# The scores multiply of an attention stage: from fp32 to two stacked fp32r halves

## The reference

```python
proj = rmsnorm(x, norm_g) @ w_in            # 1024 query columns, 48 gate columns
...
s = einsum('bghqd,bgnd->bghqn', q_c, k_cmp) * scale      # compressed
s = where(valid, s - slopes * dist, NEG)
p_cmp = softmax(s) * valid.any(-1)
...
s = einsum('bghqd,bgqkld->bghqkl', q_c, ks) * scale      # blocks
s = where(dist >= 0, s - slopes * dist, NEG)
...
s = einsum('bghqd,bgmd->bghqm', q_c, kw) * scale         # window
...
o = g_c[0] * o_cmp + g_c[1] * o_slc + g_c[2] * o_win
return out @ w_out
```

## Time and profile before

| what | value |
|---|---|
| median of 3 runs | 2514.72 us (2511.58 to 2517.59) |
| the profiled execution, its own time | 2515.49 us |
| its span | 2513.6 us, 31422 instructions |
| mean granted TensorE clock | 0.954 of full |
| busy of the span | PE 92%, PEld 70%, DVE 49%, ACT 37%, POOL 33% |
| key/value stage and attention | from about 1707 to about 2090 us of the span |

### The profile page before, as it was taken

How to read it: one execution, slowest core, us unless ns; L and a number is a source line. 1 busy time by engine, 2 the same in 40 slices (tenths; PEclk the granted TensorE clock), 3 DMA queues, 4 the chain that set the end, 5 groups by cost and what they waited for, 6 DMA issues and landing times.

```text
span 2513.6 us, 31422 instructions
## 1 busy us (share of the span) xinstructions
PE 2301.6 (92%) x10462; PEld 1770.5 (70%) x10462; DVE 1234.5 (49%) x1886; ACT 937.9 (37%) x1466; POOL 825.4 (33%) x366
## 2 busy tenths in 40 slices
PE   3899999998699999788869999999999999999997
PEld 2677777776578888655437888887655557788886
DVE  5466666643433332289964333234265565333322
ACT  4433433433444432342144443221254444444322
POOL 2522222222434444431204444445101103444442
PEclk8999999999799999989989999999699999999998
DMA  3211111112222232211102222422000001222322
GB/s 121 92 34 42 33 42 33 42 34 71 71 78 98 97 108 92 79 43 42 50 17 92 92 100 92 147 89 84 9 17 17 17 9 59 92 92 100 104 94 77
DMA packets 43689, 169.94 MB, mean 68 GB/s; under 512 B 4849, under 2 KB 4977, under 8 KB 43121
## 3 DMA queue, kind: packets, MB, share of 16 engines
q1 hardware_dynamic: 43056, 163.82, 19.5%
q10 hardware_dynamic: 576, 5.37, 0.5%
HBM read 167.08 MB, written 2.10 MB: 67 GB/s over the span
## 4 chain that ended last, share of the span: by engine, by line
PE 74%; DVE 10%; issue 9%; ACT 5%; POOL 1%; DVEq 1%; DMA 1%; ACTq 0%; POOLq 0%; SPq 0%
PE bank L282 19%; PE bank L284 19%; PE bank L283 19%; PE bank L1631 2%; PE bank L707 2%; ACT Pr L1677 2%; PE bank L699 1%; PE bank L712 1%; PE bank L1595 1%; DVE ACC L382 1%; DVE act L778 1%; PE bank L1462 1%; POOL WL L247 1%; PE bank L1613 1%; DVE Y L1365 1%
## 5 line engine op out<-in xcount | busy, mean ns | idle before, releaser
L247 POOL TENSOR_TENSOR WL<-raw,WR 128x1024 fp32r<-128x1024 f32 (+2 forms) x288 | 738.0, 2563 | 973.9 <-ACT WR L243 969.3
L282 PE MATMUL bank<-XR,WR 128*128 128x512 f32 x1528 | 631.9, 414 | 45.9 <-DVE XL L403 31.7
L284 PE MATMUL bank<-XR,WL 128*128 128x512 f32 x1528 | 603.0, 395 | 0.0
L283 PE MATMUL bank<-XL,WR 128*128 128x512 f32 x1528 | 602.0, 394 | 0.0
L243 ACT ACTIVATE WR<-raw 128x1024 fp32r<-128x1024 f32 (+2 forms) x230 | 255.7, 1114 | 739.3 <-PE bank L284 731.7
L282 PEld LDWEIGHTS bank<-XR,WR 128*128 128x128 f32 x1528 | 290.7, 190 | 123.7 <-issue 37.0
L282 PE MATMUL bank<-MR,WR 128*128 128x512 f32 (+1 forms) x856 | 336.5, 393 | 17.3 <-DVE ML L1391 8.0
L283 PEld LDWEIGHTS bank<-XL,WR 128*128 128x128 f32 x1528 | 291.9, 191 | 60.2 <-issue 7.9
L284 PEld LDWEIGHTS bank<-XR,WL 128*128 128x128 f32 x1528 | 290.6, 190 | 61.8
L283 PE MATMUL bank<-ML,WR 128*128 128x512 f32 (+1 forms) x856 | 332.9, 389 | 0.0
L284 PE MATMUL bank<-MR,WL 128*128 128x512 f32 (+1 forms) x856 | 332.8, 389 | 0.0
(11 more groups left out here) (268 smaller groups left out, 2676.6 us busy)
## 6 DMA issues: line engine op xcount, KB each, us to landing
raw<-w SPq DMA_DIRECT2D x224, 512.0 KB, 3.3
raw<-w SPq DMA_DIRECT2D x48, 704.0 KB, 4.0
raw<-w SPq DMA_DIRECT2D x16, 384.0 KB, 3.0
hT<-xT SPq DMA_DIRECT2D x1, 2048.0 KB, 8.1
hT<-xT ACTq DMA_DIRECT2D x1, 2048.0 KB, 7.8
phi<-phi ACTq DMA_DIRECT2D x1, 2048.0 KB, 8.5
out<-Y SPq DMA_DIRECT2D x8, 256.0 KB, 2.0
memT<-memT ACTq DMA_DIRECT2D x1, 1024.0 KB, 8.0
```

The source lines that it names most:

```text
L247: nc.gpsimd.tensor_tensor(WL[:, here], raw[:, here], WR[:, here].bitcast(F32), ALU.subtract).then_inc(weight_split, 1)
L282: nc.tensor.matmul(into, wr, xr(k0 + k), start=start, stop=False)
L283: nc.tensor.matmul(into, wr, xl(k0 + k), start=False, stop=False)
L284: mm = nc.tensor.matmul(into, wl, xr(k0 + k), start=False, stop=stop)
```

## The change

Lines L1407 to L1810 of the kernel. The scores multiply takes fp32r operands. A query tile is made for each pair and group, Q_S[j][g], 128 rows deep: 64 rows hold the high halves of the 64 query features, the other 64 the low halves. The keys stand doubled, once in each half of the rows, as a high tile and a low tile (KS for the full branches, KC for the compressed one). Scores are then two matmuls of 128 rows (with the high, and with the low keys) in place of one fp32 matmul of 64 rows. Q_S is made by ScalarE (two high halves, `q_scalar`) and VectorE (two low halves, `q_vector`), both behind the eviction of item 2 or 8. The key tiles are made once in the key/value stage.

The inputs to the gate and query units are multiplied by R before they are split (`q_scale` on VectorE, a high half on ScalarE, `q_low` on VectorE), so that neither the query tiles nor the gate rows need R afterwards. VectorE builds the windows before it takes the gate rows, and TensorE waits for the gate rows (tile_taken, seg_a.tile0 + 7) before the window matmuls. The gates' sigmoid and transposes move ahead of the second small layer. Buffers move to other places in SBUF.

```diff
+        KS = [[[at(f"KS{i}{g}{part}", (16 + 8 * i + 4 * g + 2 * part) * KB, SEQ, F32R) for part in range(2)]
+               for g in range(2)] for i in range(2)]
...
+            pe.wait_ge(tile_taken, seg_a.tile0 + 7)
...
-            pe.wait_ge(hid_ready, 2)
-            nc.tensor.matmul(bank[7][:, 0:32], phi2[:, 0:P], hidden[:, 0:32], start=True, stop=True)
-            nc.tensor.matmul(bank[7][0:32, 128:256], hidden[:, 32:64], phi2[:, P:2 * P], start=True, stop=True).then_inc(cmp_done, 1)
...
             pe.wait_ge(gate_sig, 1)
             for b in range(NB):
                 mm = nc.tensor.transpose(bank[2][:, b * 48:(b + 1) * 48], g_rows[0:48, b * P:(b + 1) * P], ident[0:48, 0:48])
             mm.then_inc(gate_turned, 1)
+            pe.wait_ge(hid_ready, 2)
...
-                high_part(act, "q", n, q_in_R[n], cols(hT, n), param("b_norm", n))
+                act.wait_ge(q_scaled, n + 1)
+                nc.scalar.activation(q_in_R[n], cols(SQ, n % 2), ACT.Identity).then_inc(input_high, 1)
+            act.wait_ge(unit_done, seg_a.unit0 + 6)
+            for i in range(2):
+                act.wait_ge(tile_taken, seg_a.tile0 + 3 + i)
+                for g in range(2):
+                    for rows in (HALF[g], HALF[1 - g]):
+                        nc.scalar.activation(KS[i][g][0][rows, :], k_rows[i][HALF[g], :], ACT.Identity).then_inc(keys_high, 1)
...
-            low_parts = iter(range(DT))
+
+            def q_scale(n):
+                if n >= 2:
+                    dve.wait_ge(input_ready, INPUT["q"] + n - 1)
+                V.scalar_tensor_tensor(cols(SQ, n % 2), cols(hT, n), param("b_norm", n), R[:, :], ALU.mult, ALU.mult).then_inc(q_scaled, 1)
+
+            def q_low(n):
+                dve.wait_ge(input_high, INPUT["q"] + n + 1)
+                V.tensor_tensor(q_in_L[n], cols(SQ, n % 2), q_in_R[n].bitcast(F32), ALU.subtract).then_inc(input_ready, 1)
+
+            q_scale(0)
+            q_scale(1)
...
-                for n in (next(low_parts, None), next(low_parts, None)):
-                    if n is not None:
-                        low_part(dve, "q", n, q_in_L[n], cols(hT, n), q_in_R[n], param("b_norm", n))
-            dve.wait_ge(tile_taken, seg_a.tile0 + 6)
-            dve.wait_ge(unit_done, seg_a.unit0 + 7)
-            V.tensor_tensor(g_rows[0:48, :], kv_bank(6)[0:48, :], R[0:48, :], ALU.mult).then_inc(tile_taken, 1)
+                for n in range(2 * j, 2 * j + 2):
+                    if n < DT:
+                        q_low(n)
+                        if n + 2 < DT:
+                            q_scale(n + 2)
             for i in range(2):
+                dve.wait_ge(tile_taken, seg_a.tile0 + i + 1)
                 order.link(V.memset(windows[i][:, :], 0.0))
                 out_w = windows[i][:, :].rearrange("p (l n) -> p l n", l=L_CMP)
...
+            dve.wait_ge(unit_done, seg_a.unit0 + 7)
+            V.tensor_copy(g_rows[0:48, :], kv_bank(6)[0:48, :]).then_inc(tile_taken, 1)
+            for i in range(2):
+                for g in range(2):
+                    dve.wait_ge(keys_high, 4 * i + 2 * g + 1)
+                    for rows in (HALF[g], HALF[1 - g]):
+                        V.tensor_tensor(KS[i][g][1][rows, :], k_rows[i][HALF[g], :], KS[i][g][0][HALF[g], :].bitcast(F32),
+                                        ALU.subtract).then_inc(keys_low, 1)
...
-            dve.wait_ge(cmp_done, 1)
-            V.tensor_copy(k_cmp[:, :], bank[7][:, 0:32]).then_inc(cmp_ready, 1)
-            V.tensor_copy(v_cmp[:, :], bank[7][0:32, 128:256]).then_inc(cmp_ready, 1)
...
-            pe.wait_ge(tile_taken, i * 2 + (q_tiles + j))
+            if isinstance(i, int) and i == 0 and j == 0:
+                pe.wait_ge(tile_taken, q_tiles)
+            else:
+                pe.wait_ge(q_ready, i * 4 + 2 * j)
...
-            rows = slice(64 * g, 64 * g + 64)
-            pe.wait_ge(tile_taken, i * 2 + (q_tiles + idx // N_ITEMS * 2 + j + 1))
+            pe.wait_ge(q_ready, i * 4 + (idx // N_ITEMS * 4 + 2 * j + g + 1))
             pe.wait_ge(scores_read, nth(i, idx) + 1)
...
-                    mm = nc.tensor.matmul(bank[2][:, b * 32:(b + 1) * 32], qT[j][rows, b * P:(b + 1) * P], k_cmp[rows, :],
-                                          start=True, stop=True)
+                    for part in range(2):
+                        mm = nc.tensor.matmul(bank[2][:, b * 32:(b + 1) * 32], Q_S[j][g][:, b * P:(b + 1) * P], KC[g][part][:, :],
+                                              start=part == 0, stop=part == 1)
...
-                    mm = nc.tensor.matmul(bank[2 + n][:, at0:at0 + (b + 1) * P], qT[j][rows, b * P:(b + 1) * P],
-                                          k_rows[r - 1][rows, 0:(b + 1) * P], start=True, stop=True)
+                    for part in range(2):
+                        mm = nc.tensor.matmul(bank[2 + n][:, at0:at0 + (b + 1) * P], Q_S[j][g][:, b * P:(b + 1) * P],
+                                              KS[r - 1][g][part][:, 0:(b + 1) * P], start=part == 0, stop=part == 1)
...
+            pe.wait_ge(cmp_low, 4)
             scores_tensor(pe, 0, 0)
+            pe.wait_ge(keys_low, 8)
+            pe.wait_ge(vt_ready, 2)
+            pe.wait_ge(v_cmp_ready, 1)
             scores_tensor(pe, 0, 1)
...
+        def q_scalar(act, i, j):
+            act.wait_ge(unit_done, i * 2 + (q_units + j + 1))
+            for g in range(2):
+                nc.scalar.activation(Q_S[j][g][HALF[g], :], bank[0][HALF[g], :], ACT.Identity).then_inc(q_high, 1)
...
         def q_vector(dve, i, j):
-            dve.wait_ge(unit_done, i * 2 + (q_units + j + 1))
-            nc.vector.tensor_tensor(qT[j][:, :], bank[0][:, :], R[:, :], ALU.mult).then_inc(tile_taken, 1)
+            for g in range(2):
+                dve.wait_ge(q_high, i * 4 + (2 * j + g + 1))
+                nc.vector.tensor_tensor(Q_S[j][g][HALF[1 - g], :], bank[0][HALF[g], :], Q_S[j][g][HALF[g], :].bitcast(F32),
+                                        ALU.subtract).then_inc(q_ready, 1)
...
                     evict_vector(dve, i, n)
+                    if n % 6 == 2 and exists(i, n + 6):
+                        q_vector(dve, *((i, 1) if n < 6 else (i + 1, 0)))
                     if exists(i, n + 1):
                         scale_vector(dve, i, n + 1)
                     if exists(i, n + 2):
                         read_vector(dve, i, n + 2)
-                    if n == 1:
-                        q_vector(dve, i, 1)
-                    if n == 7 and exists(i, N_ITEMS):
-                        q_vector(dve, i + 1, 0)
```

More of the change, by code:

```diff
@@ L1415, in program @@
         v_rows = [at(f"v_rows{i}", behind_r + (4 + 2 * i) * KB, SEQ) for i in range(2)]
+        KC = [[at(f"KC{g}{part}", behind_l + 128 * (2 * g + part), 32, F32R) for part in range(2)] for g in range(2)]
+        v_cmp = at("v_cmp", behind_l + 512, P, parts=32)
         v_tok = [at(f"v_tok{i}", behind_r + (8 + 2 * i) * KB, SEQ) for i in range(2)]
-        k_cmp = at("k_cmp", behind_l, 32)
-        v_cmp = at("v_cmp", behind_l + 128, P, parts=32)
-        gates = at("gates", behind_l + 640, NB * 48)
         g_rows = at("g_rows", behind_l + 2 * KB, SEQ)
         c_rows = [at(f"c_rows{i}", behind_l + (4 + 2 * i) * KB, SEQ) for i in range(2)]
+        gates = at("gates", low + 6 * KB + 32, NB * 48)
+        KS = [[[at(f"KS{i}{g}{part}", (16 + 8 * i + 4 * g + 2 * part) * KB, SEQ, F32R) for part in range(2)]
+               for g in range(2)] for i in range(2)]
         windows = [at(f"windows{i}", (32 + 4 * i) * KB, L_CMP * 32) for i in range(2)]
@@ L1471, in kv_tensor @@
             mm.then_inc(gate_turned, 1)
+            pe.wait_ge(hid_ready, 2)
+            nc.tensor.matmul(bank[7][:, 0:32], phi2[:, 0:P], hidden[:, 0:32], start=True, stop=True)
+            nc.tensor.matmul(bank[6][0:32, 128:256], hidden[:, 32:64], phi2[:, P:2 * P], start=True, stop=True).then_inc(cmp_done, 1)
         def kv_scalar(act):
@@ L1479, in kv_scalar @@
                 nc.scalar.activation(hidden[:, i * 32:(i + 1) * 32], bank[5 + i][:, 0:32], ACT.Silu).then_inc(hid_ready, 1)
-            act.wait_ge(tile_taken, seg_a.tile0 + 7)
-            nc.scalar.activation(g_rows[0:48, :], g_rows[0:48, :], ACT.Sigmoid).then_inc(gate_sig, 1)
+            act.wait_ge(cmp_done, 1)
+            for g in range(2):
+                for rows in (HALF[g], HALF[1 - g]):
+                    nc.scalar.activation(KC[g][0][rows, :], bank[7][HALF[g], 0:32], ACT.Identity).then_inc(cmp_high, 1)
         def kv_vector(dve, order):
@@ L1694, in y_scalar @@
             nc.scalar.activation(cols(MR, i * 2 + (8 + j)), bank[7][:, :], ACT.Identity).then_inc(y_high, 1)
+        def q_scalar(act, i, j):
+            act.wait_ge(unit_done, i * 2 + (q_units + j + 1))
+            for g in range(2):
+                nc.scalar.activation(Q_S[j][g][HALF[g], :], bank[0][HALF[g], :], ACT.Identity).then_inc(q_high, 1)
         def attend_scalar(act):
             alibi_scalar(act, 0, 0)
+            q_scalar(act, 0, 0)
```

(3 more changed lines are left out.)

42 lines of the change are left out of this document (26 added, 16 removed).

## The result

| | before | changed |
|---|---|---|
| median of the runs compared | 2517.74 us | 2524.11 us (2521.69 to 2536.44, 12 runs) |
| ratio, 95% interval | | 1.0036 [1.0022, 1.0049] |
| span of the profiled execution, granted clock | 2513.6 us, 0.954 | 2523.2 us, 0.947 |

The account below looks back on a forecast made before the run. VectorE's list was taken to bind the 15.36 us group, not TensorE. The span was 2513.6 - 0.1 - 4.3 + 3.5 + 6.7 = 2519.4 us, giving a forecast median of 2520.5 us, range 2507 to 2534.

Parts of the forecast that it names:

- key/value stage, to the pair unit: Making keys, windows and gates: windows +0.9, from their end to the pair unit -1.6, first pair +0.6; together -0.1 us.
- start of the attention: First work of the attention, at half clock, where TensorE binds: shorter scores give -4.3 us (ends 0 and -6).
- query halves, 7 turns: Behind each of seven pair units, making the query halves puts read(a) 0.5 us later: +3.5 us.
- clock: Weighing(a): longer TensorE waits drop the clock in six of 15 groups, four more than now, 1.68 us each: +6.7 us.
- What binds: Steady attention group of 15.36 us: VectorE's list binds; TensorE is on the path for only 3.43 us.
- TensorE bound after all: Rival, steady attention: the scores' half comes back in full, 2468 us, or half of it, about 2490; chance 0.10.
- Scores: Steady attention: scores take 1.13 to at most 1.3 us against 2.35, with 0 gained on the path.
- Compressed scores: Steady attention, ahead of weighing(a): they go from about 1.0 us to between 0.2 and 1.0, taken as 0.5.
- that sign of being right: In a steady group TensorE is idle 1.4 us or more ahead of weighing(a), ended by ACT PT.
- about 60: Sign of being right: TensorE's busy time in a steady 74 us falls to about 60 us.
- after 1755: Sign of being wrong, key/value stage: the window matmuls start before 1750 or after 1755 us.
- Nearer to the low end since each row of today shows the edge: Reason for taking six clock falls, +6.7 us, between ends of 0 of 15 (-3.4) and all (+21.8).

Follow-up runs that it names:

- c3_fill_behind: The changed kernel with four extra useless TensorE multiplies behind each weighing(c) alone; ratio to the kernel before 1.0010.
- b4_before_fill: The kernel before with three extra useless TensorE multiplies ahead of each weighing(a); ratio to the kernel before 0.9987.
- a2_before_short: The kernel before with only the scores shortened: two fp32r matmuls of 64 rows, the second overwriting the first, low halves left out; ratio 1.0014.
- a1_fill: The changed kernel with six extra useless TensorE multiplies ahead of each weighing(a) and four behind each weighing(c); ratio to the kernel before 1.0003.
- b1_qlate: The changed kernel with VectorE's low query halves moved behind the read of the same step; ratio to the kernel before 1.0040.
- b3_fill4: The changed kernel with four extra useless TensorE multiplies ahead of each weighing(a) alone; ratio to the kernel before 1.0036.
- c1_fill44: The changed kernel with four extra useless TensorE multiplies ahead of each weighing(a) and four behind each weighing(c); ratio to the kernel before 1.0012.
- c4_short_fill44: The kernel before with only the scores shortened (low halves left out), plus four extra multiplies ahead of weighing(a) and four behind weighing(c); ratio 1.0005.
- c2_qlate_fill44: The changed kernel with low query halves behind the read, plus four extra multiplies ahead of weighing(a) and four behind weighing(c); 2507.96 us, ratio 0.9973.

## Why the prediction was right, step by step

Clean group periods come from c3_fill_behind, which has no fill ahead of weighing(a) and keeps its clock in most groups: 21.45 with a pair, 15.15 without. Before: 20.79 and 15.36. The kernel before without its falls is b4_before_fill's 274.5 less 0.9 for its one slow weighing, 273.6; the changed one would be 273.6 + 7 x (0.66 - 0.21) = 276.8.

| term | forecast | measured |
|---|---|---|
| key/value stage, to the pair unit | -0.1 | -1.3 (windows +0.45, from there -1.7) |
| start of the attention | -4.3 | -5.6 |
| query halves, 7 turns | +3.5 | +3.2 |
| clock | +6.7 | (295.7 - 276.8) - (280.3 - 273.6) = +12.2 |
| sum | +5.8 | +8.5, and +1.0 of drift outside |

- *What binds*: right. VectorE's list and ScalarE's eviction set the group; less TensorE work alone gave nothing (a2_before_short), and more of it cost nothing as long as it fitted the wait: with three more multiplies b4_before_fill keeps its groups at 20.79 and 15.37. Six, in a1_fill, overshoot it and cost 0.6 and 0.44 a group (22.06 and 15.59). "TensorE bound after all" is refuted, though the page said 91% and b4_before_fill 99%.
- *Scores*: turning(b) and scores together take 1934.20 - 1931.74 = 2.46 and turning alone 1.24 (1981.62 to 1982.86), so 1.22 for the scores, as forecast (1.13 to 1.3). *Compressed scores* did not shrink: 1.06 against 1.07, where I took 0.5. Eight products of 32 columns with 128-column weights cost 0.13 each before and after, so it wasn't the passes over the columns that set it. So the idle time ahead of weighing(a) did not grow to 1.5; it is 0.97, and that sign of being right is missing. So is "about 60" for TensorE's busy time in a steady 74 us: it is 65.26 (1923.86 to 1997.86, clock 0.91), with the slow weighings in it.
- *Query halves*: +0.67 per pair group against 0.5, but 0.21 less in each other group, through the pair's split standing earlier (the last leg, 5.99 against 6.21), where I had said 0.1 at most. Most of that comes from the shorter scores, which I had put at 0: a2_before_short has 15.22 where it keeps its clock, 0.14 less than before. GpSimd did not hold them, as the row of a PSUM input had said. The Trainium skill (SBUF — State Buffer, section "SBUF: two separate sides") has the rule that a VectorE operation with both inputs in SBUF and a GpSimd operation that reads SBUF shut each other out; b1_qlate agrees, to 0.02 us.
- *Key/value stage*: the window matmuls start at 1755.78, and "after 1755" was a sign of being wrong. 3.55 of it were there before the stage began; without them it is 1752.2, as forecast (1752.7).
- *Start*: right in sign, 1.3 short. The clock is back to 1.00 at the first weighing(a) (2.37 us), which took 4.35 before; these 2.0 us stand in the clock's term.
- *Clock*: the mechanism was right, the size half of what it is. A fall costs what I took, 1.7 each (18.9 / 11, 6.7 / 4). The number failed: I counted two falls today and there were three behind the first (the third, 4.03 us, in the last turn), and took four more. Behind the first there were eight more, 11 in place of 3; the first one no longer falls, so the net is seven. "Nearer to the low end since each row of today shows the edge" was the wrong reading: standing on the edge, the place falls with the next bit of work taken away. I had named a second wait ahead of turning(a), of about 1 (it is 0.65), but counted on the one ahead of weighing(a); c3_fill_behind and b3_fill4 show that the place of the second counts more. The waits ahead of scores(b) and weighing(c) I had not seen at all. The rule of the Trainium skill (TensorE: Matmul & The Clock Gate, section "HAM oscillation — how this bites in real kernels"), by which a wait in each turn costs the clock in each turn, would have had all 15 fall: 11 did, between its 15 and my six, and the clock's 12.2 us is nearer to my 6.7 than to its 21.8. Its example waits for transfers, far longer than the 0.2 to 1.15 us of a turn here.

That the total came near is in part luck. The clock's price was half of what it is, and two things beside the right mechanism hid that: start and key/value stage gave 2.5 more than forecast against the 5.5 that the clock took more, and the medians lie 6.4 apart where the two profiled executions, from which the table is made, lie 9.5 apart.

Open: why c1_fill44 and c4_short_fill44 still fell at other places in some turns, and c2_qlate_fill44 hardly; and whether useful work can take the place of the fill. It was not tried.

## What to carry to other kernels

Walk one steady turn from mark to mark before believing that the busiest engine binds: here TensorE, 95% busy, was in 3.4 of 15.4 us of it. If it does not bind, taking work from it opens waits, and the price of those is the clock: count the slow turns of today; here four became eleven. A few useless multiplies in the waits are a one-line trial that tells what the clock costs, and may be worth keeping; count how many fit the wait, since here six cost time that four did not. And before an operation is moved out of the way, see what stall it stood in (the 1.41 us of query halves hid 1.34) and who needs its result next (moved two items on, they kept TensorE waiting 1.2 to 1.7 us).

## What the runs showed of the hardware that I had not expected

- The same line of eight multiplies takes 2.37 us, or up to 4.5, by what ran before it: thin work (weighing(c) of 32 rows, small transposes, 32-column scores) and waits of 0.3 to 1 us. 116 extra multiplies of 0.22 us in the changed kernel's stretch (c1_fill44) shorten it by 10.3 us, 144 of them (a1_fill) by 11.9 (one execution each; the ratios, 1.0012 and 1.0003 against 1.0036, have the same sign).
- A compressed-scores multiply of 32 columns took 0.13 us in fp32r over 128 rows and, of the same eight records per item, in fp32 over 64 rows. The window items went from 2.35 to 1.22 with the same step.
- A subtraction with 64 of 128 partitions takes 0.70, what 128 take (0.69).
